# Two attention stages of a float32 block: units taken two at a time on opposite partition halves, with a second output bank

## The reference, cut to what matters

```python
# even layer, 4 heads of width 2 x 64, values of width 128
logits = einsum('bqhmd,bshd->bhmqs', q, k) * dh ** -0.5 + bias      # m: two parts of a head
p = softmax(where(mask, logits, -inf))
attn = p[:, :, 0] - lam * p[:, :, 1]
o = rmsnorm(einsum('bhqs,bshe->bqhe', attn, v))
# even layer, 8 heads of width 64, keys outside the selection left out
o = einsum('bhqk,bqkhd->bqhd', softmax(q @ k_sel * dh ** -0.5 + bias), v_sel)
# odd layer, 16 heads of width 64
o = einsum('bhqk,bkhd->bqhd', softmax(q @ k * dh ** -0.5 + bias), v)
```

## Time and profile before

| What | Value |
|---|---|
| Median of 3 runs | 1701.47 us (1697.99 to 1702.29) |
| The profiled execution | 1702.13 us, span 1700.4 us |
| Mean granted TensorE clock | 0.986 of full |
| PE / PEld / DVE / ACT busy | 96% / 81% / 60% / 51% |
| Even attention stage | 808.8 to 846.1 us of the span |
| Odd attention stage | 1385.5 to 1418.8 us of the span |

### The profile page before, as it was taken

How to read it: one execution, slowest core, us unless ns; L and a number is a source line. 1 busy time by engine, 2 the same in 40 slices (tenths; PEclk the granted TensorE clock), 3 DMA queues, 4 the chain that set the end, 5 groups by cost and what they waited for, 6 DMA issues and landing times.

```text
span 1700.4 us, 20934 instructions
## 1 busy us (share of the span) xinstructions
PE 1631.2 (96%) x8484; PEld 1379.3 (81%) x8484; DVE 1026.0 (60%) x1391; ACT 864.3 (51%) x1193; POOL 23.6 (1%) x26
## 2 busy tenths in 40 slices
PE   7988988999999999999899999999999999999999
PEld 7876876899987888877777888888888878778887
DVE  5554658688846554568766655455544765765553
ACT  4364555566635443555655544354443564664442
POOL 0000002000000000000000000000000000000000
PEclk9988999999999999999999999999999999999999
DMA  7745324445454555544042645555555532535553
GB/s 274 282 149 206 148 99 149 161 177 194 176 196 159 188 179 192 177 171 158 26 163 99 246 176 197 179 188 178 188 184 182 189 124 85 188 110 188 179 192 124
DMA packets 42961, 289.96 MB, mean 171 GB/s; under 512 B 5049, under 2 KB 5199, under 8 KB 9969
## 3 DMA queue, kind: packets, MB, share of 16 engines
q1 hardware_dynamic: 38272, 271.93, 44.6%
q0 software_dynamic: 4592, 16.69, 2.9%
HBM read 287.51 MB, written 8.55 MB: 174 GB/s over the span
## 4 chain that ended last, share of the span: by engine, by line
PE 87%; DVE 6%; DMA 2%; ACT 2%; issue 1%; DVEq 1%; SPq 0%; POOL 0%; ACTq 0%
PE bank L459 26%; PE bank L461 25%; PE bank L460 25%; PE bank L465 6%; DVE low L427 2%; DMA raw<-stream_dram 2%; PE bank L729 2%; PE bank L1344 1%; ACT high L416 1%; PE bank L1655 1%; DVEq L2573 1%; PE bank L611 1%; PE bank L1851 0%; DVE stat L647 0%; DVE h L1127 0%
## 5 line engine op out<-in xcount | busy, mean ns | idle before, releaser
L427 DVE TENSOR_TENSOR low<-raw,high 128x2048 fp32r<-128x2048 f32 x255 | 582.8, 2294 | 385.0 <-ACT high L416 384.4
L416 ACT ACTIVATE high<-raw 128x2048 fp32r<-128x2048 f32 x257 | 488.8, 1913 | 372.4 <-DMA raw<-stream_dram 363.5
L459 PE MATMUL bank<-high,xh 128*128 128x512 f32 (+1 forms) x1232 | 486.9, 395 | 6.7 <-DVEq L2573 3.1
L461 PE MATMUL bank<-high,xl 128*128 128x512 f32 (+1 forms) x1232 | 478.5, 388 | 0.0
L460 PE MATMUL bank<-low,xh 128*128 128x512 f32 (+1 forms) x1232 | 478.1, 388 | 0.0
L459 PEld LDWEIGHTS bank<-high,xh 128*128 128x128 f32 x1232 | 232.9, 189 | 54.9 <-issue 3.9
L461 PEld LDWEIGHTS bank<-high,xl 128*128 128x128 f32 x1232 | 232.6, 189 | 48.7
L460 PEld LDWEIGHTS bank<-low,xh 128*128 128x128 f32 x1232 | 233.1, 189 | 44.7
L459 PE MATMUL bank<-high,hh 128*128 128x512 f32 x440 | 171.9, 391 | 0.0
L461 PE MATMUL bank<-high,hl 128*128 128x512 f32 x440 | 171.3, 389 | 0.0
L460 PE MATMUL bank<-low,hh 128*128 128x512 f32 x440 | 171.2, 389 | 0.0
(11 more groups left out here) (234 smaller groups left out, 1540.2 us busy)
## 6 DMA issues: line engine op xcount, KB each, us to landing
raw<-stream_dram SPq DMA_DIRECT2D x257, 1024.0 KB, 4.8
band_wide_dram<-band_rows_dram POOLq DMA_DIRECT2D x1, 3072.0 KB, 28.5
t_wide_dram<-t_rows_dram POOLq DMA_DIRECT2D x1, 2304.0 KB, 14.5
u<-mem_dram POOLq DMA_DIRECT2D x2, 1024.0 KB, 5.2
bias<-band_wide_dram POOLq DMA_DIRECT2D x1, 2048.0 KB, 14.6
rel_wide_dram<-rel_rows_dram POOLq DMA_DIRECT2D x1, 1920.0 KB, 15.7
bias<-t_wide_dram POOLq DMA_DIRECT2D x1, 1536.0 KB, 7.8
bias<-rel_wide_dram POOLq DMA_DIRECT2D x1, 1280.0 KB, 7.0
```

The source lines that it names most:

```text
L416: act.activation(self.high[:, n % RING, :], self.raw[:, n % RING, :], ACT.Copy).then_inc(self.high_split, 1)
L427: dve.tensor_tensor(self.low[:, n % RING, :], self.raw[:, n % RING, :], self.high[:, n % RING, :].bitcast(F32), ALU.subtract).then_inc(sel ...
L459: pe.matmul(out, lh, rh, start=start, stop=False)
L461: return pe.matmul(out, ll, rh, start=False, stop=stop)
```

## The change

Both stages now use a new class, `Twos`, which is `Paired` without streamed work between the pairs. It has two output banks, 4 and 5, used by pairs in turn; DVE's finish comes two pairs later than the logits that it stands behind, instead of one; value(i) waits for the outputs of two pairs before. 14 `keep_clock` matmuls follow the first two score pairs (16 stood there), and two more stand ahead of each later score pair, behind its wait. `Paired` itself does the same as before with its single bank.

```diff
     SCORE_BANKS = (0, 1, 6, 7)
-    OUT_BANK = 4
+    OUT_BANKS = (4,)
+    DUMMIES = 0
...
-        return self.core.bank[self.OUT_BANK][:, at:at + u.n * u.dv]
+        return self.core.bank[self.OUT_BANKS[i // 2 % len(self.OUT_BANKS)]][:, at:at + u.n * u.dv]
...
                 pe.wait_ge(s["logits_ready"], i - 2)
+                keep_clock(pe, c, self.DUMMIES, self.SCORE_BANKS[i % 4])
...
-            if i >= 2:
-                pe.wait_ge(s["out_taken"], i - i % 2)
+            if i >= 2 * len(self.OUT_BANKS):
+                pe.wait_ge(s["out_taken"], i - i % 2 + 2 - 2 * len(self.OUT_BANKS))
...
-        for i in range(0, len(units) + 2, 2):
+        late = 2 * len(self.OUT_BANKS)
+        for i in range(0, len(units) + late, 2):
             if i + 2 < len(units):
                 logits(i + 2)
                 logits(i + 3)
-            if i:
-                finish(i - 2)
-                finish(i - 1)
+            if i >= late:
+                finish(i - late)
+                finish(i - late + 1)
             self.groups.split_low(dve, i // 2 + 1)
...
+class Twos(Paired):
+    OUT_BANKS = (4, 5)
+    DUMMIES = 2
+    def __init__(self, core, units):
+        super().__init__(core, units, Dummies(core, (), None))
...
+class Dummies(Fill):
+    def tensor(self, pe, s, g):
+        if g == 0:
+            keep_clock(pe, self.core, 14, self.BANK)
...
-    st.append(Attention(c, units, fill=16))
+    st.append(Twos(c, units))
...
-    st.append(Attention(c, units, fill=16))
+    st.append(Twos(c, units))
```

## The result

The changed kernel takes 1711.1 us, median of 6 runs (1709.71 to 1711.87); the kernel before takes 1702.3 beside it (1697.99 to 1703.82, 6 runs). The ratio is 1.0054, with a 95% interval from 1.0043 to 1.0064: slower by half a per cent. The forecast was 1706.0 and its range ended at 1711.

What follows compares the result with a forecast made beforehand. PE bounds the odd stage and the even stage's front, DVE the even stage's end. -2.3 - 1.8 + 6.8 + 2.2 = +4.9 us on 1701.5, less 0.4: 1706.0 us; range 1699 to 1711.

Steps and rivals of the forecast that it cites:

- The even stage up to the last logits: Even stage's front, set by DVE: last logits end near 839.8 instead of 841.56, -1.8 us.
- its tail: Even stage behind the last logits: PE idle 4.0 us, then low clock, +6.8 us; only +2.8 at full clock.
- The stage behind the even one: Opening of the next stage: clock still low, costing half of some 4 to 5 us, +2.2 us.
- The odd stage: Whole odd stage, bound by PE: -6.8 +1.3 +1.8 +0.4 +0.6 +0.4 = -2.3 us.
- Scores: Odd stage: paired score matmuls overlap, saving 4 x 1.06 + 4 x 0.64 = 6.8 us of PE.
- Waits: Odd stage: new PE idle time for copies, 0.26 us for each of 7 pairs, 1.8; ACT last once, 0.4.
- 0.2 to the hand-overs on its two sides: Odd stage's loop: 0.2 us around the 0.60 us copy, against 0.54 of the first turn: 0.26 idle a pair.
- the dummies' +1.3: Each stage: two fewer dummies at the front, 12 more between pairs, +1.3 us of PE.
- The pairs do not overlap: Rival: 6.8 us of scores come back in the odd stage, dummies and waits stay; 1712.8 us, chance 0.02.
- The clock holds in the even tail: Rival: full clock at the even stage's end, +2.8 there; 1700.2 us, no change, chance 0.13.
- The waits do not bind: Rival: odd stage's waits and late finish hide (-5.5), even stage's end keeps its clock (-1); 1695.0 us, chance 0.08.
- The clock falls earlier too: Second of the rivals: falls also behind the even stage's first values and once in the odd stage, +3.4; 1709.5 us, chance 0.17.

Runs made afterwards that it cites:

- tail_fill: Changed kernel plus 28 dummy matmuls ahead of the last turns of the even stage, where PE waits anyway: 1704.87 us, ratio 1.0015.
- copy_first: Changed kernel with ACT taking the copies of the pair before the last ahead of the last pair's exps, in both stages: 1715.25 us, ratio 1.0069.
- no_between: Changed kernel without the two dummy matmuls ahead of each later score pair: 1707.15 us, ratio 1.0032.
- four_slots: Changed kernel with four slots for turned probabilities instead of two, by a second buffer: 1707.66 us, ratio 1.0047.
- odd_only: Changed kernel with the change kept in the odd stage alone, the even stage as in the kernel before: 1702.55 us, ratio 0.9996.
- values_first: Changed kernel with PE taking the values of the pair before ahead of the next score pair: 1711.64 us, ratio 1.0061.
- wide_tail: Changed kernel with 28 dummies ahead of the even stage's last turns and 8 ahead of the last values in both stages: 1704.93 us, ratio 1.0026.
- pairs_warm: Kernel before with scores paired in both stages, plus six dummies ahead of the values of units 10 to 14 in the even stage: 1695.23 us, ratio 0.9969.
- pair_scores: Kernel before with only the scores issued for two units at a time, into four banks, and 14 dummies at the front: 1697.32 us, ratio 0.9979.
- pairs_odd: Kernel before with only the scores paired, in the odd stage alone, the even stage unchanged: 1696.17 us, ratio 0.9972.

## Why the prediction was right or wrong

**The mechanism that decides was named, placed and nearly sized; what failed are the sizes of terms beside it.** The last logits were put at 839.8 and ended at 839.86. The last turns were put at 841.6 behind 4.0 us of idle time, and stand at 841.69 behind 4.04. The clock fell there, as the first block had shown, and the way from the last logits to the last finish, put at 11.3, took 11.6. tail_fill shows that the clock and not the wait carries most of it. Two details were off and cost little: the wait ahead of the turns before was 1.31 and not 2.9, and the clock fell in the long one alone (in copy_first, no_between and four_slots it fell around the earlier one).

**The time was 5.1 us above the forecast.** By the spans it is +9.2 us where the sum had +4.5; the 4.7 between lie in the terms below, less 0.3 ahead of the even stage, and the remaining 0.4 between profiled executions and medians. The even stage up to the last logits gained 1.4 us (31.34 for 32.73 from its first matmul) and not 1.8; its tail lost 7.1 and not 6.8. Together that is 0.7. The terms that failed are the other three:

*The stage behind the even one, +2.2 in the sum, measured +3.5.* The step was "half of some 4 to 5 us", read from the first block. Here the clock stayed low for about 9 us behind the attention, through the turns, two waits of 1.31 and 1.48 us, and twelve 512-column matmuls. I had also taken 0.4 off for an early return of the clock, which did not come. In the first block it had come back after some 4 us of that stage's work, at about 260.6; no run shows why it took longer here.

*The odd stage, -2.3 in the sum, measured -0.9.* Two terms of it were mis-sized. Scores: I counted 4 x 0.64 and 4 x 1.06 saved, 6.8 us. But the kernel before's first three units had their 12 narrow score records in 1.06 us already, where the changed kernel has 16 in 1.09:

```profile
1385.53 1.13 PE L465 MATMUL bank<-t 64*128 64x128 f32 x12 [0.98 <-DVEq L2573]
```

```profile
1394.46 1.16 PE L465 MATMUL bank<-t 64*128 64x128 f32 x16 [0.98 <-DVEq L2595]
```

By the rows of the whole stage scores took 12.7 us before (1.06, five units of 0.64, eight of 1.06) and 6.6 after (1.09, two pairs of 0.64, four of 1.06): 6.1 saved, and a row of the front was priced as if it were the average. Waits: I put 0.26 to each pair and 0.4 once for ACT, 2.2 in all. From start to start the way from values to turns is longer by 0.35 in each of three pairs (1404.61 to 1405.89 less the 0.94 of the earlier trace rows), by 0.56 in the next, by 0.2 and 0.2 in the last two, and within three pairs the second turn stands off from the first by 0.18, 0.18 and 0.45: 2.8. The failed step is "0.2 to the hand-overs on its two sides": together with the copy they take more, and they met the second turn as well as the first. The two make 1.3 of the 1.4; the dummies' +1.3 was nearly right (6 x 0.24 between the pairs, less 0.25 at the front: 1.2).

*Behind the odd stage, nothing in the sum, measured +1.2.* I priced the last finish at +0.6 and left out that the clock may fall behind it. The idle time ahead of the next stage's turns is 1.32 us instead of 0.72, and the clock fell within the 16 turns, which took 2.94:

```profile
1426.97 2.94 PE L729 MATMUL bank<-const,o 128*128 128x128 f32 x16 [1.32 <-DVEq L2595]
```

That the longer idle time is the cause is not shown. odd_only, tail_fill and values_first have the same 1.31 to 1.32 us and slow turns (3.45, 3.29 and 3.39), but no_between, four_slots and wide_tail have it too, behind the same values, and turns in 1.94. What decides stays open.

**The rivals.** "The pairs do not overlap" is dead: 1.13 us for eight in both places. "The clock holds in the even tail" is dead by the values of 6.93 us. "The waits do not bind" is dead by the idle times ahead of turns. "The clock falls earlier too" came nearest in time, 1709.5, but by another mechanism: the clock of the odd stage is 1.00, and in the even stage it fell where the forecast had it. What it had in common with the truth is that low clock costs more than the sum held; the rest of it lay behind the stages and not inside.

**What the chances missed.** Same stood at 0.48 and slower at 0.44. The forecast stood at the edge of "slower" by its own sum. The terms that the trace of before could not show (the waits of the loop, the stretch at the low clock behind the stage, what a later finish sets off) were set at or below the middle of their bounds as if each were free to err either way. They were hardly independent, since all of them have to do with longer idle times of PE, and all of them fell on the dear side. That the measured time lies only 0.1 us above the range of 1699 to 1711 is partly luck: the range reached so far up for the second rival, which did not come true.

## What to carry to other kernels

Pairing matmuls on two partition halves paid 6.2 us in a stage that PE bounds, and it needs only the scores in pairs: turning everything around it into pairs, with dummies between, gave back 5.3 of them. 1.5 came back with two more slots and 1.0 without the dummies. Where an engine is given less to do in a stage that another engine bounds, look at the longest idle stretch that results at its end and price what may follow at the low clock, the stage behind included; wide matmuls that nobody reads, put into waits that exist anyway, bought back 6.2 us with no other edit. A rate read from the steady part of a loop is not that of its first units, so count a saving row by row over the whole stage.

## What the runs showed of the hardware

The clock did not come back with work alone. In the changed kernel PE ran 32 narrow value records without a pause for 6.9 us (843.43 on) and the granted clock stayed at 0.50, the level of 1.2 GHz; the low stretch lasted some 20.5 us (840.65 to 861.1), from within the wait to the residual stage's second row of turns. In tail_fill 28 matmuls of 256 columns in the same wait, and in pairs_warm six ahead of each of five groups of values, went with a clock of 1.00 (2.4 GHz) to the end of the stage.

And it came back once where PE had just fallen idle. In values_first the clock was 0.50 through eight value records (838.20 to 840.0), 1.00 while PE stood idle for the next 2.44 us and through the eight turns behind (842.44, 1.14 us), and 0.50 again from 843.4 on, in the 32 value records.

One long wait is not needed. In pair_scores the clock fell between waits of 1.15 and 1.14 us, which have narrow values and turns between them (four value records in 0.63 us, then, behind the second wait, eight in 1.94 instead of 1.08), and in one execution of the unchanged even stage (pairs_odd) it fell behind waits of 0.74 and 0.92. In the profiled execution of the kernel before it did not fall behind the same waits (0.73 and 0.92). No run here tells what decides between the two.

Two matmuls ahead of a change of shape cost less than they last: 0.24 us for two that take 0.41 from start to start, since 0.17 of it is spent between turns and scores in any case.
